# A two-block transformer on one core: the order of copies, squares, roots, weights and half additions at five places of the last block, and eight dummy products

## What is computed

```python
h = rms_norm(x, norm1_w) * (1.0 + sc1) + sh1
z, xbc, dt_raw, q, k, v = split(h @ w_in)
y_ssd = ssd_mixer(z, xbc, dt_raw, ...)
y_sb = stick_breaking_mixer(q, k, v, q_norm_w, k_norm_w)
x = x + g1 * (concatenate([y_ssd, y_sb]) @ w_out)
h = rms_norm(x, norm2_w) * (1.0 + sc2) + sh2
x = x + g2 * ((silu(h @ w_gate) * (h @ w_up)) @ w_down)
```

## Time and profile before

| | |
|---|---|
| Median of three runs | 2231.28 us |
| The profiled execution | 2231.11 us, of which the span from the first to the last instruction is 2229.1 us |
| Mean granted TensorE clock | 0.999 of full speed |
| Norm of the last block | 1382 to 1400 us |
| V tiles | 1518 to 1588 us |
| Heads | 1595 to 1691 us |
| Pairs | 1696 to 1819 us |

### The profile page before, as it was taken

The page is one execution under the profiler, slowest core; times in us unless marked ns, Lnnn a source line. Parts: engine busy times, 40 slices in busy tenths (PEclk is TensorE's granted clock), DMA queues, the critical chain, the costliest instruction groups (busy, mean ns, idle before and its releaser), DMA issues.

```text
span 2229.1 us, 29269 instructions
## 1 busy us (share of the span) xinstructions
PE 2199.9 (99%) x10486; PEld 1768.0 (79%) x10486; DVE 1200.9 (54%) x1547; ACT 995.5 (45%) x1573; POOL 1094.1 (49%) x547
## 2 busy tenths in 40 slices
PE   7999999999999999999999999999999999999999
PEld 6877788888888877778888888887777678888887
DVE  6877874222344887775222344858887745333300
ACT  5568643222214558744333214435645654443311
POOL 4973344444443983243444443433666653444442
PEclk9999999999999999999999999999999999999999
DMA  4322122333572321123333473322221012333332
GB/s 159 94 67 67 57 95 89 100 94 95 189 234 83 97 76 57 57 85 95 94 94 95 154 238 107 104 85 64 68 87 57 29 48 83 106 94 98 100 94 85
DMA packets 59846, 216.04 MB, mean 97 GB/s; under 512 B 6640, under 2 KB 6896, under 8 KB 59760
## 3 DMA queue, kind: packets, MB, share of 16 engines
q1 hardware_dynamic: 52272, 187.62, 27.4%
q10 hardware_dynamic: 7488, 27.27, 3.6%
HBM read 212.76 MB, written 2.10 MB: 96 GB/s over the span
## 4 chain that ended last, share of the span: by engine, by line
PE 90%; DVE 4%; ACT 2%; issue 1%; POOL 1%; DMA 0%; SPq 0%; ACTq 0%; POOLq 0%; DVEq 0%
PE bank L1644 28%; PE bank L1646 27%; PE bank L1645 27%; PE bank L1867 1%; PE bank L1795 1%; ACT prob L589 1%; POOL soft_lo L416 1%; PE bank L1841 1%; PE bank L1724 1%; PE bank L1719 1%; PE bank L2150 1%; PE bank L2161 0%; DMA cst<-consts 0%; DVE conv L1213 0%; PE bank L2194 0%
## 5 line engine op out<-in xcount | busy, mean ns | idle before, releaser
L341 POOL TENSOR_TENSOR wl<-raw,wh 128x1024 fp32r<-128x1024 f32 x351 | 860.9, 2454 | 1007.9 <-ACT wh L472 1007.9
L1644 PE MATMUL bank<-hh,wh 128*128 128x512 f32 (+1 forms) x2000 | 787.4, 394 | 18.4 <-DMA cst<-consts 12.0
L1646 PE MATMUL bank<-hh,wl 128*128 128x512 f32 (+1 forms) x2000 | 772.2, 386 | 0.0
L1645 PE MATMUL bank<-hl,wh 128*128 128x512 f32 (+1 forms) x2000 | 771.5, 386 | 0.0
L472 ACT ACTIVATE wh<-raw 128x1024 fp32r<-128x1024 f32 x351 | 369.5, 1053 | 571.7 <-PE bank L1646 502.7
L1644 PEld LDWEIGHTS bank<-hh,wh 128*128 128x128 f32 x2000 | 376.4, 188 | 107.6 <-issue 14.3
L1645 PEld LDWEIGHTS bank<-hl,wh 128*128 128x128 f32 x2000 | 376.8, 188 | 78.5 <-issue 5.0
L1646 PEld LDWEIGHTS bank<-hh,wl 128*128 128x128 f32 x2000 | 376.5, 188 | 76.9
L1644 PE MATMUL bank<-ah,wh 128*128 (+1 forms) x512 | 201.7, 394 | 0.0
L1646 PE MATMUL bank<-ah,wl 128*128 (+1 forms) x512 | 200.7, 392 | 0.0
L1645 PE MATMUL bank<-al,wh 128*128 (+1 forms) x512 | 198.7, 388 | 0.0
(11 more groups left out here) (371 smaller groups left out, 2816.2 us busy)
## 6 DMA issues: line engine op xcount, KB each, us to landing
raw<-stream SPq DMA_DIRECT2D x351, 512.0 KB, 3.6
ada_w<-ada ACTq DMA_DIRECT2D x48, 512.0 KB, 4.6
x<-x_t ACTq DMA_DIRECT2D x4, 512.0 KB, 8.3
out_t<-x SPq DMA_DIRECT2D x8, 256.0 KB, 2.1
cst<-consts SPq DMA_DIRECT2D x1, 640.0 KB, 5.0
tmp<-masks SPq DMA_DIRECT2D x1, 320.0 KB, 5.3
par<-params SPq DMA_DIRECT2D x1, 253.0 KB, 6.3
cst<-consts SPq DMA_DIRECT2D x1, 224.0 KB, 9.8
```

The source lines that it names most:

```text
L341: nc.gpsimd.tensor_tensor(wl[:, slot, :], raw[:, raw_slot, :], wh[:, slot, :].bitcast(F32), ALU.subtract).then_inc(lo_ready, 1)
L1644: mm(dst, wh[:, slot, w], xh, start=start, stop=False)
L1645: mm(dst, wh[:, slot, w], xl, start=False, stop=False)
L1646: return mm(dst, wl[:, slot, w], xh, start=False, stop=stop)
```

## The change

In the heads, TensorE's sums of heads 2 to 6 move to the third group of the tile after next, that of head 7 to the seventh group of tile 8 as before; ScalarE's roots of heads 2 to 6 are taken one step later, that of head 7 in step 8 as before. In the V tiles, the copy of tile 0 moves ahead of the exponentials of pair 1, and each rounding is called apart from the copy (in the first step it stays behind the exponentials). In the first pair, ScalarE takes the weights of the later keys between the logarithms of head 0 and head 1. In the last pair, one block of three products moves between the high and the low sums of the first keys. In the norm's gap, the half addition of tile 7 moves behind the first low part, ScalarE's squares behind its second copy, and TensorE gets eight products of 256 columns whose result is not used.

```diff
--- before.py
+++ after.py
@@ -282,8 +282,8 @@
         across = [tmp[:, 4, :], tmp[:, 5, :]]
 
 
-        SQUARES_IN = {0: {}, 1: {}, 2: {6: 0}, 3: {3: 1, 6: 2}} | {i: {6: i - 1} for i in range(4, 16)}
-        ROOTS_AT = {0: [], 1: [], 2: [0], 3: [1, 2]} | {i: [i - 1] for i in range(4, 16)}
+        SQUARES_IN = {0: {}, 1: {}, 2: {6: 0}, 3: {3: 1}} | {i: {2: i - 2} for i in range(4, 8)} | {8: {2: 6, 6: 7}} | {i: {6: i - 1} for i in range(9, 16)}
+        ROOTS_AT = {0: [], 1: []} | {i: [i - 2] for i in range(2, 8)} | {8: [6, 7]} | {i: [i - 1] for i in range(9, 16)}
         NORMS_AT = {0: [], 1: [], 2: [0, 1]} | {i: [i - 1] for i in range(3, 16)}
         HEAD_BANK = [4 + j % 4 if j < 12 else 4 + j % 2 for j in range(16)]
         HEAD_FREE = {j: j - 3 if j < 14 else j - 1 for j in range(4, 16)} | {12: 9, 13: 10}
@@ -735,7 +735,7 @@
                 h, t = u // KT, u % KT
                 act.wait_ge(xn_ready, u + 1)
                 af(hh[:, t, half_cols[h]], norm1_shift[u % 4], ACT.Copy).then_inc(hh_ready, 1)
-                if u == 0:
+                if u == 1:
                     act.wait_ge(x_new, XN)
                     norm1_square(6, half_cols[1])
                     norm1_square(7, half_cols[1]).then_inc(sq_ready, 1)
@@ -803,7 +803,6 @@
                 if t >= 2:
                     act.wait_ge(v2_turned, t - 1)
                 af(v_tmp[t % 2][:, :], bank[:, 6, :], ACT.Copy).then_inc(v2_copied, 1)
-                round_chunk(CB + B_V + t + RW)
 
             def put_v(t):
                 act.wait_ge(v2_turned, t + 1)
@@ -812,9 +811,13 @@
                 last.then_inc(v2_out, 1)
 
             for t in range(1, KT):
+                if t == 1:
+                    copy_v(0)
                 exp_within(t)
                 exp_across(t)
-                copy_v(t - 1)
+                if t > 1:
+                    copy_v(t - 1)
+                round_chunk(CB + B_V + t - 1 + RW)
                 if t == KT - 1:
                     y_root(0)
                 if t == 1:
@@ -822,6 +825,7 @@
                 put_v(t - 1)
                 y_square(t - 1)
             copy_v(KT - 1)
+            round_chunk(CB + B_V + KT - 1 + RW)
             y_square(KT - 1)
             def head_square(i):
                 item, src = SB + S_HEADS + i, q2[:, i, :] if i < 8 else k2[:, i - 8, :]
@@ -857,8 +861,8 @@
                 af(oh[:, t, :], bank[:, 7, :], ACT.Copy).then_inc(oh_ready, 1)
 
             act.preload_act_table_set("natural_log_exp_and_others")
-            def log_of(t, p):
-                for heads in [(0,), (1,)] if p else [(0, 1)]:
+            def log_of(t, p, sets):
+                for heads in sets:
                     for e in heads:
                         act.wait_ge(abs_ready, piece(t, p, e) + 1)
                         af(log1p[e][:, part_at[p]], log1p[e][:, part_at[p]], ACT.Exp, scale=-1.0).then_inc(log_exp, 1)
@@ -871,16 +875,18 @@
                     act.wait_ge(cum_ready, piece(t, p, e) + 1)
                     af(weight[:, e, part_at[p]], logit[e][p], ACT.Exp).then_inc(weight_ready, 1)
 
-            log_of(0, 0)
+            log_of(0, 0, [(0, 1)])
             for t in range(PAIRS):
-                log_of(t, 1)
+                log_of(t, 1, [(0,), (1,)] if t else [(0,)])
                 if t:
                     act.wait_ge(o_ready, t)
                 weights(t, 0)
+                if t == 0:
+                    log_of(t, 1, [(1,)])
                 if t:
                     heads_out(t - 1)
                 if t + 1 < PAIRS:
-                    log_of(t + 1, 0)
+                    log_of(t + 1, 0, [(0, 1)])
                 weights(t, 1)
                 for i in range(len(ssd_blocks(t))):
                     m = ssd_tile_after(t, i)
@@ -1323,8 +1329,6 @@
                     add_norm1_square(5)
                     dve.wait_ge(down_ready, (KT - 1) * (l + 1))
                     half_added(6, 1).then_inc(x_new, 1)
-                    dve.wait_ge(used, c0 + C_LAYER)
-                    half_added(7, 1).then_inc(x_new, 1)
                 else:
                     down_added(0)
                     down_added(1)
@@ -1353,6 +1357,9 @@
             norm1_shifted(1)
             for u in range(2 * KT):
                 norm1_rest(u)
+                if u == 0:
+                    dve.wait_ge(used, CB)
+                    half_added(7, 1).then_inc(x_new, 1)
                 if u + 2 < 2 * KT:
                     norm1_shifted(u + 2)
             for h in range(2):
@@ -1945,6 +1952,9 @@
             pe.wait_ge(x_down_half, 2)
             for end in last_two(7, T // 2, T // 2):
                 end.then_inc(used, 1)
+            pe.wait_ge(x_new, XN - 1)
+            for _ in range(8):
+                mm(norm1_sum[1], wh[:, (CB + 1) % RW, 0:P], wh[:, (CB + 1) % RW, 0:T // 2], start=True, stop=True)
 
             def lin(c, m, before=lambda kk: None):
                 pe.wait_ge(lin_free, m - 3)
@@ -2154,7 +2164,7 @@
                         last = mm(flat[:, at:at + P], ident_bf[:, :], diag_mask[:, :], start=False, stop=True, skip_group_check=True)
                     last.then_inc(logit_ready, 1)
 
-            def later_sums(t, p, e):
+            def later_sums(t, p, e, beside=lambda: None):
 
                 def within(j, src):
                     at, n = SB_BANK[e][j], T - j * P
@@ -2179,6 +2189,7 @@
                 sums = first_keys if p else last_keys
                 pe.wait_ge(soft_ready, piece(t, p, e) + 1)
                 sums(soft_hi[:, e, :])
+                beside()
                 pe.wait_ge(soft_split, piece(t, p, e) + 1)
                 sums(soft_lo[:, e, :]).then_inc(cum_ready, 1)
 
@@ -2210,14 +2221,17 @@
                     pe.wait_ge(sums_ready, 1)
                 later_sums(t, 0, 0)
                 later_sums(t, 0, 1)
-                for n in blocks[-2:]:
-                    ssd_block(n)
+                ssd_block(blocks[-2])
                 if t + 1 < PAIRS:
+                    ssd_block(blocks[-1])
                     logits(t + 1, 0)
                 beside = 0 if ssd_tile_after(t, 5) is not None else 1
                 for n in ahead[0:beside]:
                     ssd_block(n)
-                later_sums(t, 1, 0)
+                if t + 1 < PAIRS:
+                    later_sums(t, 1, 0)
+                else:
+                    later_sums(t, 1, 0, lambda: ssd_block(blocks[-1]))
                 later_sums(t, 1, 1)
                 for n in ahead[beside:]:
                     ssd_block(n)
```

## The result

The changed kernel takes 2238.14 us (median of seven runs, 2237.56 to 2239.46), the kernel before 2231.30 us beside it (seven runs, 2230.97 to 2232.12): a ratio of 1.0032, 95% interval 1.0021 to 1.0042. It is slower by 0.3%, and the forecast of 2238.0 us holds. The profiled execution took 2237.56 us, its span is 2235.7 us.

What follows compares the result with a forecast made beforehand. TensorE, busy 99% of the span, bounds the kernel. The parts sum -0.1 - 1.0 + 7.7 + 0.3 + 0 = +6.9 us on 2231.1 us: 2238.0 us, own range 2236.0 to 2240.0, whole range 2230.5 to 2241.0 us.

Steps and rivals of the forecast that it cites:

- The heads: Heads: late roots make a VectorE-ScalarE loop slower than TensorE's 5.95 us tile; +7.7 us, bounds -1.6 and +9.4.
- the turn: Heads: one pass of squares, rounding, root, reciprocal and scaling through ScalarE and VectorE takes 7.53 us, paid five times.
- VectorE's wait: Heads: VectorE idles some 2.7 us ahead of the reciprocals of heads 2 to 6, until ScalarE's root.
- the waits at sums 4 to 7: Heads: TensorE waits 0.6 us at square sum 4, 1.5 each at 5 and 6, 4.3 at 7.
- some 9 us: Heads: TensorE's waits at the square sums grow to this in all, with 1.5 us at sum 8.
- Rival 1: Heads: roots come in time at VectorE's reciprocal, result not slower; 2228.7 us, or 2225.9 us; chance 0.17.
- The V tiles: V tiles: most of the 2.1 us copy wait moves one tile later; -1.0 us, bounds -3.8 and +0.3.
- rival 3: V tiles: ScalarE pays another 1.4 us at the table load; 2239.4 us; chance 0.02.
- Rival 2: Clock falls in new waits: 1.7 us at V, up to 1.7 at heads, mostly hidden; 2239.7 to 2241.4 us; chance 0.20.
- First pair: First pair: logits start earlier, but GpSimd's low halves come 0.35 us later; +0.3 us, bounds -1.7 and +0.85.
- Last pair: Last pair: the moved block fills a wait and empties as much ahead of it; 0 us, bounds -0.7 and +0.7.
- The norm: Norm's gap: second half's root does not move, dummies give nothing back; -0.1 us, bounds -0.5 and +0.4.

Runs made afterwards that it cites:

- Experiment 1: Kernel before with only the new tables of the heads (sums of heads 2 to 6 later, roots one step later): 2239.28 us, ratio 1.0035.
- 2: Changed kernel with the old table of roots, sums left where the change puts them: 2228.99 us, ratio to before 0.9992.
- 4: Changed kernel with VectorE's reciprocal and scaling of heads 2 to 6 put later too: 2231.94 us, ratio 1.0003.
- 9: Changed kernel with ScalarE's rounding in steps 3 to 7 put behind the root that follows: 2234.54 us, ratio to before 1.0014.
- 7: Kernel before with the first-pair edit alone (weights of the later keys between the two heads' logarithms): 2231.26 us, ratio 1.0001.
- 8: Kernel before with the last-pair edit alone (one block of three products between high and low sums): 2231.09 us, ratio 0.9999.
- 5: Kernel before with the norm edits alone (half addition and squares moved, eight dummy products): 2231.02 us, ratio 0.9997.
- 6: Kernel before with the V-tile edits alone (copy of tile 0 ahead of the exponentials, roundings apart): 2231.12 us, ratio 1.0000.
- 10: Changed kernel without the eight dummy products in the norm's gap: 2238.06 us.

## Why the prediction was right

**The heads** decided, and each piece stood: the turn 7.53 us forecast and 7.46 measured, VectorE's wait 2.7 and 2.71, the waits at sums 4 to 7 of 0.6, 1.5, 1.5 and 4.3 us against 0.45, 1.26, 1.31 and 4.01, the part +7.7 and +7.64. (The forecast's list of waits adds up to 8.0 us and not to the 7.8 beside it: 0.6 + 3 x 1.5 + 4.3 - 1.4.) The "some 9 us" of waits at the sums came out as 7.0, because the wait at sum 8 is missing: there TensorE lost its time at half clock instead (below). Experiment 1 shows that it is this edit, 2 that it is the roots, 4 that the loop closes through VectorE, 9 that the turn is a plain sum. Rival 1, with roots in time, fell.

**The V tiles**: -1.0 forecast, -1.19 measured, by the forecast's own steps. Timeline of the changed kernel, against the earlier trace rows:

```profile
1523.75 0.60 ACT L805 ACTIVATE root<-bank 128x512 f32<-128x512 f32 x1 [2.37 <-PE bank L1653]
1524.37 1.28 ACT L772 ACT_TABLE_LOAD   x1
1525.66 1.15 ACT L772 ACTIVATE cst<-cst 128x512 f32<-128x512 f32 x2
...
1529.51 2.27 DVE L1454 TENSOR_TENSOR z<-z,xc 128x512 f32<-128x512 f32 x1
...
1528.87 0.74 PE L2016 MATMUL bank<-running_split,block_sum 128*128 128x512 f32 x2 [0.52 <-DVE tmp L1473]
...
1536.18 0.47 PE L1651 MATMUL bank<-hh,wh 128*128 128x512 f32 x1 [1.71 <-ACT acs_t L805]
```

The load stands between copy and exponentials, the running sum waits 0.52 us (0.4 forecast), the copy of tile 1 is waited for 1.71 us (1.9). But the -1.0 holds only against an execution in which the clock fell behind the V wait, as in the one that the forecast read, and there lies some luck. In kernels 1, 7 and 8 it fell in the norm, and against them the V tiles of the changed kernel are 0.35 to 0.40 us longer and its norm 1.4 us shorter. Norm and V tiles together take 188.8 to 189.0 us in the four kernels with both old orders (before, 1, 7, 8), wherever the clock fell, and 187.85 us in the changed kernel: about -1.0 us either way. The forecast's -0.1 and -1.0 met this without having seen the second way.

There is no drain: copy, load and exponential follow each other within 0.02 us, so rival 3 fell. The Trainium skill's page "ScalarE: Activation LUTs", section "What ACT_TABLE_LOAD costs", adds 1.38 us of drain to a switch of tables; these rows show the 1.28 us alone. Rival 2 fell here too: the clock stayed at 1.00 behind the new wait. Windows of the changed kernel, against the earlier trace rows:

```profile
1386.31:1389.72 3.41, 3.33 (x24) 3.01 (x24) 3.29 (x9) 3.10 (x8) 0.00 (x0) 1.00 0.00 0
1536.18:1539.60 3.42, 3.42 (x16) 2.77 (x17) 3.39 (x3) 0.81 (x1) 2.40 (x1) 1.00 0.02 5
1647.43:1650.85 3.42, 3.42 (x9) 2.63 (x8) 3.38 (x2) 0.66 (x1) 1.67 (x1) 0.50 0.17 36
```

Behind the norm's gap and the V wait it is 1.00. The third window is the rival's other half: the clock does fall behind the 4.01 us at sum 7. TensorE waits again at sum 8 in the kernel of the forecast; with the slow stretch it no longer does (only four waits are listed): GpSimd's low half of head 8 is out at 1654.26 and TensorE takes it at 1654.53, so the fall cost about 0.3 us, hidden for the most part, as the rival's "against" had it. In experiment 1, where it lasted 6.8 us, the heads took 1.26 us more.

**First pair**: +0.3 forecast, +0.48 measured, since two low halves are waited for and not one. TensorE's timeline in the changed kernel, against the earlier trace rows:

```profile
1717.12 0.67 PE L2171 MATMUL bank<-soft_lo,later_sum 128*128 128x512 f32 x2 [1.52 <-POOL soft_lo L416]
...
1719.40 0.67 PE L2171 MATMUL bank<-soft_lo,later_sum 128*128 128x512 f32 x2 [0.63 <-POOL soft_lo L416]
```

**Last pair**: 0 and 0.

**The norm**: -0.1 forecast, +0.08 measured, with TensorE back 0.37 us behind the dummies and VectorE still held by the root of the second half. Timeline of the changed kernel, against the earlier trace rows:

```profile
1384.83 1.11 PE L1957 MATMUL bank<-wh 128*128 128x256 f32 x8
1386.31 0.39 PE L1651 MATMUL bank<-hh,wh 128*128 128x256 f32 x1 [0.37 <-DVE hl L1354]
...
1392.52 0.49 DVE L1349 SCALAR_TENSOR_TENSOR bank<-bank,mod,xg 128x256 f32<-128x256 f32 x1 [0.74 <-issue]
```

One step was wrong, without harm to the sum: "The clock is 1.00 here already, so they give nothing back". That was read from one execution, in which it had stayed. In four of the five profiles with the old order it fell here and cost 1.4 us, three times the bound given for a gain.

## What to carry to other kernels

When an instruction moves in an engine's list, write down the loops that it closes with the lists that did not move: add up one turn, compare it with the pitch of the bound engine, and multiply the excess by the turns. When a producer is put later (here the root), its consumer on the other engine has to be put later with it (experiment 4), or the producer has to stay (experiment 2); one row of a table decided 9 us here. A clock level seen in one execution is a sample, so an edit that shortens a wait of 1.8 us is better judged from several.

## What the runs showed of the hardware

The clock was less regular than expected. With the old V order (before, 1, 5, 7, 8) it fell either behind the norm's wait of 1.8 us (three times) or behind the V wait of 2.1 us (twice, both where the norm had been spared), never at both, at a price of 1.4 to 1.5 us in the one and 1.5 to 1.7 us in the other. So in the profiles the norm edit alone had the fall at the V wait (5), the V edit alone had it in the norm (6), and the eight kernels with both had it in neither. It is not a rule for every execution: three of the eleven runs of kernel 5 have a mean clock of 1.000 and took 2228.7 to 2229.0 us, 2 us less than its median. The clock stayed at 1.00 behind a wait of 1.3 us in the norm (one profile) and behind those of 1.5 to 1.7 us for V tile 1 (nine profiles). In the first pair it fell in five of fourteen, for 0.66 to 0.75 us, with either order and behind waits of 1.5 to 1.7 us. In the heads it fell at waits of 4.0 us (1, 10 and the changed kernel) and 2.1 us (4). But it stayed at 1.00 behind the longest wait of kernel 9, 3.04 us at sum 7. Its row in TensorE's timeline, and the window behind it:

```profile
1643.78 0.47 PE L2116 MATMUL bank<-square_hi,block_sum 128*128 128x512 f32 x1 [3.04 <-POOL square_lo L393]
...
1643.78:1647.20 3.42, 3.42 (x15) 2.81 (x16) 3.38 (x3) 1.64 (x2) 0.97 (x1) 1.00 0.00 0
```

So the length of the wait alone does not decide: 1.8 us was enough in four profiles, and 3.04 us was not in another. What decides in a given execution stays open; no run here tells it.
